# Two expert stages: the up matrices of pairs 5 to 14 are loaded from ScalarE's queue instead of SyncE's

## The reference

```python
def moe_ffn(h, w_rg, b_rg, w_re, b_re, w_gate, w_up, w_down):
    ...   # each token picks 2 experts of one group of 8; tokens sorted by expert
    xb = h[row_tok].reshape(n_blocks, MOE_BLOCK, d)
    def expert_block(args):
        xblk, e = args
        hid = jax.nn.silu(xblk @ w_gate[e]) * (xblk @ w_up[e])
        return hid @ w_down[e]
    yb = lax.map(expert_block, (xb, block_e)).reshape(n_rows, d)
    return jnp.zeros_like(h).at[row_tok].add(yb * row_w[:, None])
```

## Time and profile before

| | us |
|---|---|
| median of 3 runs | 1931.34 (1930.67 to 1933.36) |
| the profiled execution | 1930.34 |
| its span | 1928.6 |
| TensorE busy | 1841.9 (96%) |
| VectorE busy | 573.1 (30%) |
| ScalarE busy | 362.0 (19%) |
| DMA queue q1 | 588.74 MB, 74.7% of 16 engines' span |
| DMA queue q10 | 2.10 MB, 0.3% |

### The profile page before, as it was taken

The page is one execution under the profiler, slowest core; times in us unless marked ns, Lnnn a source line. Parts: engine busy times, 40 slices in busy tenths (PEclk is TensorE's granted clock), DMA queues, the critical chain, the costliest instruction groups (busy, mean ns, idle before and its releaser), DMA issues.

```text
span 1928.6 us, 23014 instructions
## 1 busy us (share of the span) xinstructions
PE 1841.9 (96%) x9422; PEld 1193.9 (62%) x9422; DVE 573.1 (30%) x1298; ACT 362.0 (19%) x809; POOL 12.9 (1%) x27
## 2 busy tenths in 40 slices
PE   8999999999999999999999888889999999988888
PEld 7798888857988888575454333335885444333333
DVE  3279550432755603523111011113223111110112
ACT  3440000322301003423211111112013211110111
POOL 1000000000001000000000000000000000000000
PEclk9999999999999999999999999999999999999999
DMA  9746675532377752138999999999547999999996
GB/s 299 268 175 264 275 306 225 198 119 88 141 313 290 308 196 104 67 115 363 424 428 428 428 429 429 429 428 427 203 153 281 421 428 428 429 429 428 428 429 262
DMA packets 52885, 592.02 MB, mean 307 GB/s; under 512 B 6578, under 2 KB 15034, under 8 KB 17218
## 3 DMA queue, kind: packets, MB, share of 16 engines
q1 hardware_dynamic: 52226, 588.74, 74.7%
q10 hardware_dynamic: 576, 2.10, 0.3%
HBM read 585.34 MB, written 1.05 MB: 304 GB/s over the span
## 4 chain that ended last, share of the span: by engine, by line
PE 73%; DMA 23%; DVE 2%; ACT 1%; issue 1%; SPq 0%; DVEq 0%
PE ps L495 27%; PE ps L1193 13%; DMA ring<-in_w_gate 11%; DMA ring<-in_w_up 10%; PE ps L736 8%; PE ps L1302 5%; PE ps L1154 3%; PE ps L1147 2%; PE ps L565 2%; PE ps L782 1%; DMA ring<-in_w_down 1%; PE ps L654 1%; PE ps L583 1%; PE ps L597 1%; PE ps L943 1%; PE ps L1356 1%
## 5 line engine op out<-in xcount | busy, mean ns | idle before, releaser
L1193 PE MATMUL ps<-ring,work 128*64 128x512 f32 x2048 | 458.5, 595 | 59.7 <-DMA ring<-in_w_up 38.2
L495 PE MATMUL ps<-hsq,ring 128*128 128x256 f32 x2048 | 447.3, 380 | 0.8 <-DVE hsq L2018 0.8
L495 PEld LDWEIGHTS ps<-hsq,ring 128*128 128x128 f32 x2048 | 387.8, 190 | 59.5 <-issue 7.0
L1193 PEld LDWEIGHTS ps<-ring,work 128*64 128x64 f32 x2048 | 146.5, 137 | 359.8 <-issue 300.4
L1585 ACT ACTIVATE work<-ps 128x512 f32<-128x512 f32 (+2 forms) x175 | 89.7, 517 | 844.3 <-PE ps L495 324.8
L1302 PE MATMUL ps<-ring,work 128*64 128x512 f32 x992 | 220.0, 595 | 1.7 <-DVE work L2505 1.6
L1302 PEld LDWEIGHTS ps<-ring,work 128*64 128x64 f32 x992 | 68.5, 137 | 135.0 <-issue 130.9
L736 PE MATMUL ps<-work,ring 128*128 128x256 f32 (+1 forms) x704 | 148.6, 373 | 0.0
L1963 DVE SCALAR_TENSOR_TENSOR work<-ring,silu_c,work 128x512 f32<-128x512 f32 x196 | 144.1, 755 | 5.1
L736 PEld LDWEIGHTS ps<-work,ring 128*128 128x128 f32 x704 | 130.5, 190 | 18.7 <-issue 1.7
L2457 DVE TENSOR_TENSOR work<-ps,work 128x512 f32<-128x512 f32 x26 | 18.0, 691 | 405.2 <-ACT work L1585 405.2
(11 more groups left out here) (326 smaller groups left out, 1233.4 us busy)
## 6 DMA issues: line engine op xcount, KB each, us to landing
ring<-in_w_gate SPq DMA_DIRECT2D x64, 2048.0 KB, 20.5
ring<-in_w_up SPq DMA_DIRECT2D x64, 2048.0 KB, 20.7
ring<-in_w_down SPq DMA_DIRECT2D x62, 2048.0 KB, 22.7
ring<-in_w_ada SPq DMA_DIRECT2D x24, 2048.0 KB, 8.5
ring<-in_w_ff_gate SPq DMA_DIRECT2D x10, 2048.0 KB, 13.3
ring<-in_w_ff_up SPq DMA_DIRECT2D x10, 2048.0 KB, 13.3
ring<-in_w_ff_down SPq DMA_DIRECT2D x8, 2048.0 KB, 13.8
ring<-in_ml_w_in SPq DMA_DIRECT2D x6, 2048.0 KB, 10.8
```

Of the source, the lines that this page charges most:

```text
L495: last = mm(ps[:, b, 0:T], w[:, k, m * P:(m + 1) * P], rhs[:, k, :], start=(i == 0), stop=(i == nk - 1))
L1193: last = mm(ps[e * CAP:(e + 1) * CAP, w, :], xg[:, k, e * CAP:(e + 1) * CAP], row_tile(first, w, e, k), start=(k == 0), stop=(k == last_k) ...
```

## The change

In each expert stage, SyncE no longer issues the up loads of pairs 5 to 14. ScalarE issues them, right after its wait on `up_full` and ahead of the row copies. The up loads of pairs 1 to 4 and of pair 15 stay on SyncE. SyncE's loop is cut accordingly: pairs 3 and 4 are written out, and the loop begins at pair 5 and has gate and down only. The slots, the semaphores and the bytes are the same; TensorE's and VectorE's instructions are not touched.

```diff
@@ SyncE, pairs of gathered tokens
-                    with sp.Fori(0, NEXP // 2 - 4) as i:
+                    for pair in range(3, BLOCKS + 1):
                         for w in range(2):
-                            sp.wait_ge(freed[w], i + 3)
-                            load_pair(w, i + 3)
-                        later_down(i + 3)
+                            sp.wait_ge(freed[w], pair)
+                            load_pair(w, pair)
+                        later_down(pair)
+                    with sp.Fori(BLOCKS + 1, NEXP // 2 - 1) as i:
+                        sp.wait_ge(freed[0], i)
+                        load_pair(0, i)
+                        later_down(i)
@@ ScalarE, experts
-                    with act.Fori(BLOCKS, NEXP // 2 - 1) as i:
+                    def later_pair(i, loads):
                         gate_out(i)
                         act.wait_ge(e_["up_full"], i + 1)
+                        for part in range(2 * loads):
+                            s = (moe_first[l] + 2 + part) % RING
+                            act.dma_start(ring[:, s, :], a["w_up"][l, i + 1, part]).then_inc(slot_loaded[s], 16)
                         windows(i + 1)
                         rows_out(i)
+
+                    with act.Fori(BLOCKS, NEXP // 2 - 2) as i:
+                        later_pair(i, True)
+                    later_pair(NEXP // 2 - 2, False)
                     gate_out(NEXP // 2 - 1)
                     rows_out(NEXP // 2 - 1)
```

## The result

The changed kernel takes 1938.32 us (median of 7 runs, 1937.34 to 1940.24), the kernel before, beside it, 1931.67 us (1930.67 to 1933.79). The ratio is 1.0035, 95% interval 1.0026 to 1.0044: +6.65 us. The forecast was 1936.8. The profiled execution takes 1938.32 us too (before: 1930.34), its span is 1936.5 us, its mean granted clock of TensorE 0.987 of full speed (before: 0.998).

The account below looks back on a forecast made before the run. DMA bandwidth was taken to bound the expert stages' second-half periods; stage ends cost 2.9 + 2.9 − 0.3 = +5.5 us, other terms 0, giving 1935.8 us from the profiled execution, 1936.8 on the median, range 1930 to 1947.

Parts of the forecast that it names:

- What bounds the kernel, and the issue: Second half of both expert stages: DMA bandwidth sets the 29.36 us period; issuing up on ScalarE costs 0.
- rival C: The 20 periods: two queues fill gaps one leaves, −4.6 us; 1926.7 us if overtaking costs little; chance 0.09.
- The order of transfer: Pairs 5 to 14: two queues alternate packets, so up loads overtake the second gate part by 7.2 us.
- one nor two whole loads: By the Trainium skill's rule whole 2 MB loads take turns: gate delay 4.89 or 9.79 us instead of 7.2.
- up waits no more: Mid-stage periods: TensorE stops waiting for up; the whole 4.34 us is waited at the second gate part.
- What it costs, and where: Nothing in mid-stage; at each stage's end +2.9 us, less 0.3 in the second; together +5.5 us.
- upper bound of the forecast: Per stage, both up parts wholly ahead of the gate part: 9.79 − 4.34 = +5.45 us.
- Rival A: Expert stages: order does not matter, bytes bound and the last pair catches up; 0, 1931.3 us; chance 0.22.
- Rival B: Mid-stage periods: up becomes the bound, its loop outgrowing 29.36 us; about +14 us, 1945; chance 0.12.
- the order's 2.9 us: End of the first stage: pair 14's late gate part delays the chain, 7.2 + 25.02 − 29.36 = +2.9 us.
- margin of 1.9 us for the up loop: Mid-stage periods: the up loop, with 23.8 us from issue to landing, wants 27.5 us, under 29.36 by 1.9.
- the 2.6 us of the forecast: End of the second stage: +2.9 us for order, less 0.3 absorbed by a wait in the last down product.

Follow-up runs that it names:

- e4_one_queue: Against the kernel before: from pair 5 on ScalarE issues all expert-stage loads and the next six, in the old order on one queue; 1930.54 us, ratio 1.0000.
- e2_only14: Against the kernel before: only pair 14's two up loads per stage issued by ScalarE; 1942.11 us, ratio 1.0071.
- e9_again: The changed kernel, nothing altered, profiled and timed once more; 1940.21 us, ratio to the kernel before 1.0040.
- e6_fill: Against the changed kernel: 14 extra 128x128 TensorE products between the gate product's halves in pairs 5 to 14; 1938.50 us, ratio to the kernel before 1.0037.
- e1_to12: Against the changed kernel: up loads of pairs 13 and 14 back on SyncE's queue; 1931.72 us, ratio to the kernel before 1.0004.
- e8_part0: Against the changed kernel: in pairs 5 to 14 only the first up part on ScalarE's queue, the second on SyncE's; 1933.29 us, ratio to the kernel before 1.0004.
- e7_late4: Against the kernel before: fifteen extra 128x128 TensorE products at the end of the first expert stage, all loads on SyncE; 1935.03 us, ratio 1.0020.
- e3_warm: Against the changed kernel: six extra 128x128 TensorE products between the gate product's halves in pairs 5 to 14; 1938.76 us, ratio to the kernel before 1.0045.

## Why the prediction was right

**What bounds the kernel, and the issue.** Right. Rate 428 in both, ScalarE's issues covered, nothing lost by them (e4_one_queue with three times as many), and no gain in rate (rival C).

**The order of transfer.** Right. Packets go turn by turn (54.3 and 46.9% in e2_only14), up overtakes gate, and pair 14's gate part comes 7.3 us late, counted from pair 5's start (1284.17 − 1277.22 + 0.32), for the 7.2 worked out, and neither one nor two whole loads (4.89 or 9.79). It is 7.3 us in e9_again too. In the second stage it is 5.8 and 6.6 us in these two profiles and 7.5 with filler (e6_fill), so a fit to 0.1 us is closer than the working deserves. The reading that up waits no more, and that the whole 4.34 us is waited at the second gate part in each period, does not hold: up waits 4.4 us in nine periods, and the wait at gate goes from nothing (pairs 8 and 12) to 5.4 us. The period is 29.36 us on average only.

**What it costs, and where.** Right, and the sharpest of the tests: only the last pairs count. Without 13 and 14 the cost is nil (e1_to12), with 14 alone it is 5.4 us a stage (upper bound of the forecast: 5.45), and one part in place of two, 4.89 us against the 4.34 that are free, costs nothing that can be told (e8_part0). Rival A, that order does not matter, is right for eight pairs of ten and wrong for the stage's end. Rival B did not come up in the periods: from pair 7's second gate part to pair 11's (1078.48 to 1196.03) one is 29.39 us. Its mechanism, up as what comes last, did at the end of the second stage (below).

**The sum: 5.5 forecast, 6.65 measured, and a term that was missing.** The forecast had no place for TensorE's clock. In stage 1 the order's 2.9 us has 1.4 beside it: the wait before pair 14's gate part is 5.4 us long, the clock goes to 0.50, and the product behind it is on the chain (11.93 for 10.52 us). That explains 4.3. A second 2 us falls between the stages, by a clock of 0.50 too, but with no long wait ahead of it. The Trainium skill ("TensorE: Matmul & The Clock Gate", "Part 1: The HAM clock gate" and "HAM oscillation") says that idle time throttles the array to half rate and that DMA waits can do this in each tile; the trace agrees, with 5.4 us of idle ahead of both 0.50 windows inside the first stage, while the waits of 1.3 us before the change left the clock at 1.00. Concentrating three short waits in one long one is what the change did to the clock, and I had the 4.34 us on the page without asking this of it.

In stage 2 the same terms give 2.6 to 4.0; the two profiles show 1.4 and 3.8. The chain there, first in the changed kernel's first profile and then in e9_again, goes another way than the forecast had it:

```profile
1844.14 11.85 PE ps L1193 x48
...
1856.66 23.00 DMA ring<-in_w_up
...
1879.71 3.65 PE ps L1193 x16
```

```profile
1847.31 13.06 PE ps L1193 x48
...
1861.04 22.84 DMA ring<-in_w_up
...
1883.93 3.65 PE ps L1193 x16
```

Pair 13's product behind its long wait for gate (4.20 and 6.19 us) runs in part at half clock, 11.85 and 13.06 us instead of 10.52; the up loads are issued behind it and land 23.5 and 23.4 us after their issue (forecast: 23.8); and pair 14's second up part is what TensorE waits for last. It comes 3.5 and 5.9 us late, counted from pair 5 (before: 1870.13 − 1601.10), and 2.1 us of that go into waits that the kernel before has in and behind pair 15. That leaves 1.4 and 3.8. So the forecast's "up does not wait any more" had a margin of 1.9 us for the up loop, and a product 1.3 or 2.5 us slower takes most or all of it. With the clock held up (e6_fill) the gate part is what comes last, 7.5 us late, and the stage costs the 2.6 us of the forecast. Why pair 13's wait is 4.20 us once and 6.19 us the other time I can't say.

So the mechanism was right, in the second stage only as long as the clock is held up, and the nearness of the sum is in part luck: in the first profile 3.5 us of clock and gap were missing from it (1.4 in stage 1, 2.1 between), and stage 2 cost 1.2 us less than forecast.

**Open.** Why the clock falls between the stages in four profiles and not in the eight others. Lateness does not sort them: the gather's product with the fall starts at 1464.1, 1464.5, 1466.3 and 1468.7 us, and without it at 1465.2 (e6_fill), 1465.7 (e2_only14) and 1466.9 (e7_late4) among others. The clock's own share of the loss is read from the rows, 1.4 and 2 us of the 7.9 in the first profile; e6_fill took it away only together with a cost of its own, so it isn't shown by a time.

## What to carry to other kernels

Where loads are the bound and queue several deep, the queue's order is a schedule: a second queue is a licence to overtake, here at half the rate from some 3 us after the issue. Ask what the overtaken load is needed for, and look at the end of the stage; in the middle a bound of bytes forgives it. Where a change merges waits, even at the same sum, look at what the longest one does to TensorE's clock, and at which load is issued behind the product that then runs slower.

## What the runs showed of the hardware

- Two queues share packet by packet, at an unchanged total: 54.3 and 46.9% of the engines' time while both are full, 428 to 431 GB/s.
- The clock of TensorE fell to 0.50 after waits of 5.4 us, in e3_warm also with 3.7 us of wait behind 1.6 us of filler, in the changed kernel also after 2.96 us (0.68 over the next 5.4 us) and in e8_part0 after waits of 2.6 us, though not after each of them. After waits of 1.3 us it did not fall. In e6_fill, with 3.39 us of filler and waits of 1.7 us at most, it stayed at full speed through both stages.
- Runs of one kernel spread with the clock: of the 23 runs of the kernel before beside e1 to e4, those with a mean clock of 0.998 take 1929.25 to 1930.69 us, those with 0.995 1934.39 and 1935.05 us. That is the larger part of a spread of 5.8 us, and some 1.5 us for 0.001 of mean clock. It holds where TensorE is what the kernel waits for: e1_to12 has 0.987 to 0.989 and takes 1931.72 us, since its clock falls where the loads are the bound.
